# Two transformer blocks on one core: the lower parts of the feed-forwards' inner activations start at another address

## What is computed

```python
def swiglu(x, w_gate, w_up, w_down):
    return (jax.nn.silu(x @ w_gate) * (x @ w_up)) @ w_down
...
def first_block(...):
    f1 = swiglu(rms_norm(h, ffn1_pre_g[l]), ffn1_w_gate[l], ffn1_w_up[l], ffn1_w_down[l])
    h = h + 0.5 * rms_norm(f1, ffn1_post_g[l])
    mix = hybrid_mixer(...)
    h = h + rms_norm(mix, mix_post_g[l])
    f2 = swiglu(rms_norm(h, ffn2_pre_g[l]), ffn2_w_gate[l], ffn2_w_up[l], ffn2_w_down[l])
...
def conv_ffn(h, w_up, conv_w, w_down):
    a, g = jnp.split(dwconv(h @ w_up, conv_w), 2, axis=-1)
    return (jax.nn.silu(g) * a) @ w_down
```

## The kernel before

| part | shift in elements, k = 0, 1, 2 | bytes modulo 256 |
|---|---|---|
| upper weights (`ring_hi`) | 0, 0, 0 | 0 |
| lower weights (`ring_lo`) | 16, 16, 16 | 64 |
| upper input (`u_hi`) and upper inner (`hidden_hi`) | 112, 112, 112 | 192 |
| lower input (`u_lo`) | 16, 80, 80 | 64 |
| lower inner (`hidden_lo`) | 144, 144, 208 | 64 |

## Time and profile before

### The profile page before, as it was taken

The page is one execution under the profiler, slowest core; times in us unless marked ns, Lnnn a source line. Parts: engine busy times, 40 slices in busy tenths (PEclk is TensorE's granted clock), DMA queues, the critical chain, the costliest instruction groups (busy, mean ns, idle before and its releaser), DMA issues.

```text
span 1206.9 us, 24404 instructions
## 1 busy us (share of the span) xinstructions
PE 1178.4 (98%) x9128; PEld 1111.1 (92%) x9128; DVE 816.0 (68%) x1121; ACT 637.3 (53%) x1018; POOL 527.1 (44%) x285
## 2 busy tenths in 40 slices
PE   6999999999999999999999999999999999999998
PEld 6999999987889899999999879987877999999998
DVE  7788875856865577777654852688836596655555
ACT  6444446525762555454546546468517635655553
POOL 0343436732465533343436645458530483232331
PEclk9999998999999999999989999999999999999999
DMA  6888884543334467878614333233323254666663
GB/s 221 277 278 294 283 280 130 190 140 123 105 108 137 157 210 259 292 274 292 188 52 158 123 99 129 88 106 105 105 70 106 88 175 140 208 185 188 188 189 121
DMA packets 58100, 207.10 MB, mean 172 GB/s; under 512 B 6576, under 2 KB 8240, under 8 KB 57776
## 3 DMA queue, kind: packets, MB, share of 16 engines
q1 hardware_dynamic: 49824, 177.23, 45.2%
q0 software_dynamic: 6912, 25.17, 5.7%
q10 hardware_dynamic: 1296, 3.74, 0.9%
HBM read 205.07 MB, written 1.05 MB: 171 GB/s over the span
## 4 chain that ended last, share of the span: by engine, by line
PE 82%; DVE 8%; issue 3%; ACT 3%; POOL 2%; DMA 1%; DVEq 0%; SPq 0%; POOLq 0%; ACTq 0%
PE psum L641 23%; PE psum L642 23%; PE psum L643 22%; POOL own_parts L2944 2%; PE psum L789 1%; PE psum L1017 1%; PE psum L942 1%; PE psum L652 1%; PE psum L654 1%; PE psum L653 1%; PE psum L666 1%; PE psum L1346 1%; POOL high L3039 1%; DVE u_parts L2882 1%; PE psum L700 1%
## 5 line engine op out<-in xcount | busy, mean ns | idle before, releaser
L641 PE MATMUL psum<-parts 128*128 128x256 f32 x1584 | 441.0, 278 | 14.0 <-DVE parts L2197 10.4
L642 PE MATMUL psum<-parts 128*128 128x256 f32 x1584 | 445.7, 281 | 0.0
L643 PE MATMUL psum<-parts 128*128 128x256 f32 x1584 | 441.6, 279 | 0.0
L641 PEld LDWEIGHTS psum<-parts 128*128 128x128 f32 x1584 | 299.5, 189 | 14.9 <-issue 11.0
L2952 POOL TENSOR_TENSOR parts<-low,parts 128x1024 fp32r<-128x1024 f32 x60 | 151.0, 2517 | 367.4 <-ACT parts L1520 367.4
L643 PEld LDWEIGHTS psum<-parts 128*128 128x128 f32 x1584 | 299.7, 189 | 0.0
L642 PEld LDWEIGHTS psum<-parts 128*128 128x128 f32 x1584 | 299.7, 189 | 0.0
L1520 ACT ACTIVATE parts<-low 128x1024 fp32r<-128x1024 f32 x198 | 207.4, 1056 | 163.1 <-DMA low<-stream 162.4
L2944 POOL TENSOR_TENSOR own_parts<-low,parts 128x1024 fp32r<-128x1024 f32 x75 | 184.9, 2479 | 151.5 <-ACT parts L1598 147.4
L2197 DVE TENSOR_TENSOR parts<-low,parts 128x1024 fp32r<-128x1024 f32 x138 | 163.6, 1219 | 23.6 <-ACT parts L1520 22.9
L642 PE MATMUL psum<-u_parts,parts 128*128 128x256 f32 (+1 forms) x560 | 164.7, 294 | 0.0
(11 more groups left out here) (384 smaller groups left out, 2091.1 us busy)
## 6 DMA issues: line engine op xcount, KB each, us to landing
low<-stream SPq DMA_DIRECT2D x334, 512.0 KB, 3.6
high<-conditioning POOLq DMA_DIRECT2D x48, 512.0 KB, 5.0
high<-wuq ACTq DMA_DIRECT2D x1, 1152.0 KB, 5.1
low<-x SPq DMA_DIRECT2D x4, 256.0 KB, 6.3
high<-ctx ACTq DMA_DIRECT2D x1, 1024.0 KB, 6.4
out<-low SPq DMA_DIRECT2D x8, 128.0 KB, 1.8
low<-cst ACTq DMA_DIRECT2D x1, 850.5 KB, 4.8
low<-vec ACTq DMA_DIRECT2D x1, 157.5 KB, 6.3
```

The lines of the kernel that those rows point to most:

```text
L641: pe.matmul(out, w_hi[:, cols_], x_hi, start=start, stop=False, **kw)
L642: pe.matmul(out, w_hi[:, cols_], x_lo, start=False, stop=False, **kw)
L643: return pe.matmul(out, w_lo[:, cols_], x_hi, start=False, stop=stop, **kw)
```

## The change

The three sets of shifts become one. The lower input's shift is 16 elements in all feed-forwards (before: 16, 80 and 80), and the lower inner part's is 128 (before: 144, 144 and 208). In bytes modulo 256 the lower input stays at 64 and the lower inner part goes from 64 to 0. The other shifts keep their values. The lists over k are gone, so that each part is one view in place of three. On every engine the instructions, their order and their waits are the same as before; only addresses of operands differ.

```diff
-PART_STARTS = ({"ring_lo": 16, "u_hi": 112, "u_lo": 16, "hidden_hi": 112, "hidden_lo": 144},
-               {"ring_lo": 16, "u_hi": 112, "u_lo": 80, "hidden_hi": 112, "hidden_lo": 144},
-               {"ring_lo": 16, "u_hi": 112, "u_lo": 80, "hidden_hi": 112, "hidden_lo": 208})
+PART_START = {"ring_lo": 16, "u_lo": 16, "u_hi": 112, "hidden_hi": 112, "hidden_lo": 128}
...
         def ffn_parts(name, n, width):
 
-            return [parts[:, PARTS[name][0] + starts.get(name, 0):PARTS[name][0] + starts.get(name, 0) + n * width]
-                    .rearrange("p (a b) -> p a b", a=n) for starts in PART_STARTS]
-
-        ring_hi = parts[:, 0:RING * TILE].rearrange("p (a b) -> p a b", a=RING)
-        ring_lo = ffn_parts("ring_lo", RING, TILE)
+            at = PARTS[name][0] + PART_START.get(name, 0)
+            return parts[:, at:at + n * width].rearrange("p (a b) -> p a b", a=n)
+
+        ring_hi, ring_lo = ffn_parts("ring_hi", RING, TILE), ffn_parts("ring_lo", RING, TILE)
...
                         mm = split_product(acc[n], w, slice(n * P, (n + 1) * P),
-                                           (hidden_hi[k][:, par, :], hidden_lo[k][:, par, :]),
+                                           (hidden_hi[:, par, :], hidden_lo[:, par, :]),
                                            first and n % 2 == 0, last, skip_group_check=True)
...
                 dve.wait_ge(S("hidden_upper"), count + 1)
-                dve.tensor_tensor(hidden_lo[k][:, par, :], hidden[:, par, :], hidden_hi[k][:, par, :],
+                dve.tensor_tensor(hidden_lo[:, par, :], hidden[:, par, :], hidden_hi[:, par, :],
                                   ALU.subtract).then_inc(S("hidden_split"), 1)
```

More of the change, by code:

```diff
@@ L635, in split_tile @@
                     pe.wait_ge(S("lower_ready"), more * 4 + ((3 * FC - LOWERS_2) * k + j + 1 - max(0, (j - 8) // 3 + 1)))
-                return ring_hi[:, j % RING, :], ring_lo[k][:, j % RING, :]
+                return ring_hi[:, j % RING, :], ring_lo[:, j % RING, :]
             def split_product(out, w, cols_, x, start, stop, **kw):
@@ L717, in gate_up @@
                             mm = split_product(half_bank(PJ[par], a), w, slice(c_ * P, (c_ + 1) * P),
-                                               (u_hi[k][:, c_, :], u_lo[k][:, c_, :]),
+                                               (u_hi[:, c_, :], u_lo[:, c_, :]),
                                                c_ == 0, c_ == DC - 1)
@@ L732, in gate_up_first @@
                             mm = split_product(half_bank(PJ[0], a), split_tile(k, a), slice(c_ * P, (c_ + 1) * P),
-                                               (u_hi[k][:, c_, :], u_lo[k][:, c_, :]), c_ == 0 and a == 0, c_ == DC - 1,
+                                               (u_hi[:, c_, :], u_lo[:, c_, :]), c_ == 0 and a == 0, c_ == DC - 1,
                                                skip_group_check=True)
@@ L1505, in input_upper @@
             def input_upper(k, n, g):
-                act.activation(u_hi[k][:, n, :], h[:, n, :], ACT.Identity, scale=v(g, n)).then_inc(S("input_upper"), 1)
+                act.activation(u_hi[:, n, :], h[:, n, :], ACT.Identity, scale=v(g, n)).then_inc(S("input_upper"), 1)
             def uppers(k, first, last):
@@ L1525, in upper_hidden @@
                 act.wait_ge(S("hidden_ready"), count + 1)
-                act.activation(hidden_hi[k][:, par, :], hidden[:, par, :], ACT.Copy)\
+                act.activation(hidden_hi[:, par, :], hidden[:, par, :], ACT.Copy)\
                    .then_inc(S("hidden_upper"), 1)
@@ L2113, in _ @@
                 act.wait_ge(S("prescaled"), 16 + n + 1)
-                act.activation(u_hi[2][:, n, :], u1[:, n, :], ACT.Identity, bias=modc[:, 24 + n, 0:1])\
+                act.activation(u_hi[:, n, :], u1[:, n, :], ACT.Identity, bias=modc[:, 24 + n, 0:1])\
                    .then_inc(S("input_upper"), 1)
@@ L2196, in lower @@
                 dve.wait_ge(S("upper_ready"), more * RING + (3 * FC * k + j + 1))
-                dve.tensor_tensor(ring_lo[k][:, j % RING, :], ring[:, t % RING, :], ring_hi[:, j % RING, :],
+                dve.tensor_tensor(ring_lo[:, j % RING, :], ring[:, t % RING, :], ring_hi[:, j % RING, :],
                                   ALU.subtract).then_inc(S("lower_ready"), 1)
@@ L2208, in lower_input @@
                 dve.wait_ge(S("input_upper"), DC * k + n + 1)
-                dve.scalar_tensor_tensor(out=u_lo[k][:, n, :], in0=h[:, n, :], scalar=v(g, n), in1=u_hi[k][:, n, :],
+                dve.scalar_tensor_tensor(out=u_lo[:, n, :], in0=h[:, n, :], scalar=v(g, n), in1=u_hi[:, n, :],
                                          op0=ALU.mult, op1=ALU.subtract).then_inc(S("input_split"), 1)
@@ L2214, in lower_shifted @@
                 dve.wait_ge(S("input_upper"), DC * 2 + n + 1)
-                dve.scalar_tensor_tensor(out=u_lo[2][:, n, :], in0=u1[:, n, :], scalar=modc[:, 24 + n, 0:1],
-                                         in1=u_hi[2][:, n, :], op0=ALU.add, op1=ALU.subtract)\
+                dve.scalar_tensor_tensor(out=u_lo[:, n, :], in0=u1[:, n, :], scalar=modc[:, 24 + n, 0:1],
+                                         in1=u_hi[:, n, :], op0=ALU.add, op1=ALU.subtract)\
                    .then_inc(S("input_split"), 1)
@@ L2951, in lower @@
                 pool.wait_ge(S("upper_ready"), more * RING + (3 * FC * k + j + 1))
-                pool.tensor_tensor(ring_lo[k][:, j % RING, :], ring[:, t % RING, :], ring_hi[:, j % RING, :],
+                pool.tensor_tensor(ring_lo[:, j % RING, :], ring[:, t % RING, :], ring_hi[:, j % RING, :],
                                    ALU.subtract).then_inc(S("lower_ready_2"), 1)
```

## The result

Twenty runs of the changed kernel took 1209.81 to 1214.41 us, median 1211.96 us; twenty of the kernel before took 1203.14 to 1214.74 us, median 1207.68 us (the 1211.1 us that stood ahead of the prediction was the median of the first three of these). The ratio is 1.0027, with a 95% interval of 1.0015 to 1.0040: the change makes the kernel slower by about 3.3 us. The time lies in the range that I gave, and the loss is under 0.5%, but the forecast was no change, and the whole interval lies above 1.

What follows compares the result with a forecast made beforehand. TensorE in the feed-forwards was taken as the bound. Lower input, writes and lower inner part in down at 0 us each, put on the 1211.1 us median, gave 1211.1 us, range 1205 to 1215 us.

Steps and rivals of the forecast that it cites:

- no change: Likeliest case for the whole kernel: the time stays at 1211.1 us; chance 0.45.
- What bounds the kernel: In the feed-forwards TensorE is busy throughout at full clock, so a nanosecond on its matmuls counts; no size of its own.
- The lower input: Feed-forwards k = 1 and 2: its address falls by 256 bytes and keeps its remainder, worth 0 us.
- The writes: VectorE's write of the lower inner part at its new address: 0 us, upper end about 1 us.
- The lower inner part in down: 528 down triples, L642's moved operand from remainder 64 to 0: 0 us, between -3.5 and +3.4 us.
- the slow rhythm in down: Rival, down tiles alone: 6.4 ns more in each of 528 triples, +3.4 us, 1214.5 us; chance 0.25.
- The rhythm carried into gate and up: Rival, 1056 gate and up triples also change rhythm: 1221.3 us slow (chance 0.04) or 1200.5 us quick (chance 0.03).
- The rule of the Trainium skill: TensorE's read ports for moving operand and weight loads are independent, so the change's sum would be exactly 0 us.

Runs made afterwards that it cites:

- the inner part back: Changed kernel with the lower inner part back at remainder 64 (shift 144 in all three feed-forwards); ratio to the kernel before 1.0005 (0.9982 to 1.0029).
- the lower weights at 0: Against the changed kernel, all lower weights at remainder 0, lower input at 0, lower inner part at 192; down took 2.73 us, gate and up 5.72 us.
- the input moved too: Changed kernel with the lower input at remainder 0 as well (shift 64); ratio to the kernel before 1.0081 (1.0058 to 1.0105).
- all parts alike: Against the changed kernel, lower weights at remainder 0 like the upper weights, all four activation parts at 192; ratio to the kernel before 1.0025 (1.0002 to 1.0048).

## Why the prediction was wrong

**What bounds the kernel: right.** TensorE in the feed-forwards is the bound, and no wait came in: the matmuls of the feed-forwards have no more idle time than before (13.5 us, before 14.0).

**The lower input: right.** 0 us; with the inner part back, the rhythm is 1300 to 1301 matmuls in 150 us.

**The writes: right.** `lower_hidden` takes 424 to 1529 ns (before 424 to 1526), and TensorE waited for it once, for 0.2 us, as in the earlier trace rows.

**The lower inner part in down: the step that failed.** I had 0 us between ends of -3.5 and +3.4 us, because L641 and L643 "keep their addresses and enter each down tile out of an unchanged gate and up rhythm", and because the branch products' L642 with exactly the new remainders differs by 1 ns. The second half was right and did not matter: L642 kept its 118 ns. The first half is the error. Keeping the address did not keep the time: L641 went from 113.4 to 119.2 ns and L643 from 115.0 to about 117.6. I priced the matmul whose operand moves; the runs show that the triple has to be priced as one, since a place that one operand takes changes the distance at which its neighbours run. The term measured 528 x 8 ns = 4.2 us in down and some 1056 x 1 ns = 1.1 us in gate and up, 5.3 us together by the trace, which is outside its ends.

The rival named *the slow rhythm in down* came true, with the right place and sign. Its price was 6.4 ns a triple by the branch products; measured were about 8 ns in down, and about 1 ns a triple on average in gate and up, from the first few triples behind each down tile. It had a chance of 0.25, and the trace gave it more. In the branch products of the trace before, of 88 distances from one L641 to the next that are clear of waits, 86 are 353 or 354 ns and two are 340; the window of the earlier trace rows made the quick rhythm look less rare than it is. And the earlier trace rows has L641 at 281 ns in the median where the earlier trace rows has 276: I compared L642 alone, with its 281 against 280. I set these products aside because their upper parts differ. For the rhythm's exact value that was fair (355 against 353 ns, and one rhythm against two). That they gave the right sign is in part luck: down tiles with the lower weights at 0 have the same distances of 64 bytes between moved and loaded operand, and they ran at 340 ns.

**The time itself: luck.** The forecast of 1211.1 us is within 0.9 us of the measured median, because the three runs it was built on had a median 3.4 us above that of all twenty, about as much as the change costs.

**The rhythm carried into gate and up: rightly unlikely.** 5.56 against 5.55 us.

**The rule of the Trainium skill**, page "SBUF — State Buffer", section "Who interferes with whom", that TensorE's two read ports are independent, gave 0 us. The runs disagree with 0 us: with instructions, order and waits the same, other start addresses gave 340 to 363 ns a triple. The measurement decides. Whether it is the two ports that meet, or something else behind them, no run shows.

**The size.** The trace's steady rhythm gives 5.3 us, the ratio 1.8 to 4.8 us. The same lies in the other pairs: the feed-forwards with the input moved too are 14.1 us longer by their first and last matmuls (190.7 + 192.6 + 188.1 against 186.7 + 186.9 + 183.7 us), and the ratio says 9.8 us. In the two profiles the difference lies between the feed-forwards. Stretches around the pauses behind the first and the second, before and then after the change (columns as above):

```profile
180.00:240.00 60.00, 59.20 (x475) 0.91 0.51 166
590.00:640.00 50.00, 49.43 (x403) 0.93 0.26 82
```

```profile
180.00:240.00 60.00, 59.16 (x481) 0.94 0.52 166
590.00:640.00 50.00, 49.72 (x416) 0.97 0.27 86
```

The granted clock falls from 2.4 to 1.2 GHz there: before the change TensorE ran 50 matmuls in the 9 us from 197 to 206 us, where the first feed-forward ends, and the mean clock of these 9 us was 0.66. It was low for less of the changed kernel's execution: 60 x 0.03 + 50 x 0.04 = 3.8 us less of full clock lost. But the kernel with the inner part back, whose feed-forwards are those of before, had 0.94 and 1.00 there. So these stretches differ from execution to execution, and whether slower feed-forwards shorten them is not shown. Over many runs the clock covers little of the gap: its mean over whole executions was 0.9898 in the twenty runs of the changed kernel and 0.9894 in 75 of the kernel before, a difference of 0.5 us. With the input moved too it was 0.9918 in six runs against 0.9893 in the 17 beside them, 3.0 us of the 4.3 that are missing there. The rest stays open.

## What to carry to other kernels

Here the place of one operand set the pace of the matmuls beside it. So price the whole repeating group, by start-to-start distances over all its repetitions in the trace, and compare every matmul of the group with the nearest rows, not only the one that is edited. Where such rows show two values and nothing between, as the branch products did with 353 and 340 ns, a forecast in the middle is one that no row shows. After a change of addresses, count matmuls in a stretch where the bound engine never idles; a loss of 1% of the rate showed there in a single profile, while the runs' own scatter needed twenty of them. An arrangement that runs quick in a few tiles may have a second rhythm, and then the start of the tile decides, so see whether it holds over the whole kernel.

## What the runs showed that had not been expected

- With the same instructions, a triple takes 340, 347, 353, 355, 357 or up to 363 ns on average, depending on the start addresses modulo 256 bytes and, for some sets of addresses, on the moment at which the rhythm begins; shifts by 256 bytes, of the lower input in two feed-forwards and of the lower inner part in the third, changed nothing.
- Some sets of addresses return to one rhythm whatever the start (346.7 ns before, about 355 ns after the change); with all parts alike there are two, 340 and 353 ns, each of which lasts for as long as nothing interrupts it, 1276 or 1326 matmuls in 150 us.
- A single extra matmul of 128 to 172 columns turned one rhythm into the other in most of its places; one of 192 columns did not.
- Which relation between the five addresses makes a triple quick was not found: the two simple rules that fit before and after were both refuted, and an order of reads that would explain all the kernels was not worked out.
